# The beginning of a hybrid decoder step: input rows in one queue, cached pages gathered ahead of the memory turns, queries rotated by transfers

## What is computed

```python
xn = rmsnorm(x, g_attn)
cq, ckv, kr, ... = split(xn @ w_in)          # query and key-value compressions, rotary key, ...
q = (rmsnorm(cq, g_q) @ w_uq)                # 8 heads x (128 + 64)
q_rope = rope(q[..., 128:], pos)             # x1*cos - x2*sin, x1*sin + x2*cos
q_lat = einsum('bshn,rhn->bshr', q[..., :128], w_uk)
c_kv, k_rope = rmsnorm(ckv, g_kv), rope(kr, pos)
# sample tokens attend over 2048 cached positions each, found through page_table
past_lat, past_rope = cache_lat[page_table], cache_rope[page_table]
mem_k, mem_v = rmsnorm(mem, g_mem) @ w_mk, rmsnorm(mem, g_mem) @ w_mv
# ... a gated linear recurrence, cross attention to mem_k, mem_v, then 32 experts (top 4 of 32)
```

## Time and profile before

| | us |
|---|---|
| median of 3 runs (lowest, highest) | 1360.05 (1359.65, 1361.78) |
| the profiled execution's own time | 1358.12 |
| its span, from the first instruction to the last | 1356.3 |
| PE busy | 1304.1 (96%) |
| DVE busy | 364.0 (27%) |
| ACT busy | 253.4 (19%) |
| POOL busy | 101.4 (7%) |

### The profile page before, as it was taken

The page is one execution under the profiler, slowest core; times in us unless marked ns, Lnnn a source line. Parts: engine busy times, 40 slices in busy tenths (PEclk is TensorE's granted clock), DMA queues, the critical chain, the costliest instruction groups (busy, mean ns, idle before and its releaser), DMA issues.

```text
span 1356.3 us, 17073 instructions
## 1 busy us (share of the span) xinstructions
PE 1304.1 (96%) x6899; PEld 692.5 (51%) x6899; DVE 364.0 (27%) x796; ACT 253.4 (19%) x566; POOL 101.4 (7%) x133
## 2 busy tenths in 40 slices
PE   9999999999999999999998998989999998998988
PEld 7848887788887344344243433424434343342433
DVE  3864433211456222113021111202212112120212
ACT  4314345221125111011110101101011011010102
POOL 2652221001200000000000000000000000000000
PEclk9999999999999999999999989999999999999999
DMA  9894567548969999999999999999999999999996
GB/s 325 285 363 156 202 242 246 197 145 309 293 234 377 389 417 426 429 428 429 428 429 429 429 428 428 428 429 423 430 428 430 427 430 428 431 427 428 430 425 263
DMA packets 64898, 499.03 MB, mean 368 GB/s; under 512 B 5967, under 2 KB 7352, under 8 KB 39768
## 3 DMA queue, kind: packets, MB, share of 16 engines
q1 hardware_dynamic: 51424, 453.37, 81.1%
q0 software_dynamic: 13216, 44.50, 9.7%
q10 hardware_dynamic: 216, 0.58, 0.1%
HBM read 491.34 MB, written 7.08 MB: 367 GB/s over the span
## 4 chain that ended last, share of the span: by engine, by line
PE 75%; DMA 20%; DVE 1%; POOL 1%; issue 1%; SPq 0%; ACT 0%; ACTq 0%; DVEq 0%; POOLq 0%
PE bank L1348 22%; PE bank L804 17%; PE bank L1368 13%; DMA arena<-in_w_down 10%; DMA ring<-in_w_gate_up 9%; PE bank L1401 4%; PE bank L1332 4%; PE bank L754 1%; PE bank L1357 1%; PE bank L838 1%; PE bank L1363 1%; PE bank L1285 1%; PE bank L1182 1%; PE bank L767 1%; DMA ring<-in_cache_kv_latent,arena 1%
## 5 line engine op out<-in xcount | busy, mean ns | idle before, releaser
L1348 PE MATMUL bank<-ring,arena 128*64 128x512 f32 x1536 | 344.8, 597 | 6.4 <-DMA ring<-in_w_gate_up 6.4
L1368 PE MATMUL bank<-arena 128*64 128x512 f32 x1000 | 229.3, 609 | 30.2 <-DMA arena<-in_w_down 30.2
L804 PE MATMUL bank<-arena,ring 128*128 128x264 f32 x1008 | 230.7, 388 | 0.0
L1348 PEld LDWEIGHTS bank<-ring,arena 128*64 128x64 f32 x1536 | 104.3, 137 | 222.4 <-issue 206.9
L804 PEld LDWEIGHTS bank<-arena,ring 128*128 128x128 f32 x1008 | 189.4, 190 | 36.0 <-issue 4.4
L1368 PEld LDWEIGHTS bank<-arena 128*64 128x64 f32 x1000 | 70.4, 140 | 173.9 <-issue 129.0
L2607 DVE TENSOR_TENSOR resid<-resid,bank 128x264 f32<-128x264 f32 x128 | 54.8, 429 | 355.0 <-PE bank L1401 353.5
L1348 PE MATMUL bank<-arena 128*64 128x512 f32 x512 | 115.5, 593 | 3.5 <-DMA arena<-in_w_gate_up 3.5
L2612 DVE TENSOR_SCALAR arena<-bank 128x512 f32<-128x512 f32 x32 | 22.0, 688 | 340.8 <-PE bank L1348 340.8
L1566 ACT ACTIVATE arena<-bank 128x264 f32<-128x264 f32 (+6 forms) x129 | 51.0, 403 | 165.9 <-PE bank L804 126.8
L1946 ACT COPY arena<-bank 64x512 f32<-64x512 f32 x63 | 36.5, 580 | 232.9 <-PE bank L1368 232.1
(11 more groups left out here) (364 smaller groups left out, 933.2 us busy)
## 6 DMA issues: line engine op xcount, KB each, us to landing
ring<-in_w_gate_up SPq DMA_DIRECT2D x94, 2048.0 KB, 28.9
arena<-in_w_down SPq DMA_DIRECT2D x62, 2048.0 KB, 22.2
arena<-in_w_gate_up SPq DMA_DIRECT2D x32, 2048.0 KB, 28.8
ring<-in_w_in SPq DMA_DIRECT2D x10, 2048.0 KB, 11.4
out<-arena POOLq DMA_DIRECT2D x8, 512.0 KB, 5.0
ring<-v_rows POOLq DMA_DIRECT2D x8, 512.0 KB, 6.0
ring<-in_w_o_mla SPq DMA_DIRECT2D x2, 2048.0 KB, 8.9
ring<-in_w_o_gla SPq DMA_DIRECT2D x2, 2048.0 KB, 15.2
```

Of the source, the lines that this page charges most:

```text
L804: mm = nc.tensor.matmul(lin_bank(name)[0:m, 0:width], w(ring_name, nk, cols)[:, k, a:a + m], rhs[:, k, 0:width], start=(k == 0), stop=(k = ...
L1348: mm = nc.tensor.matmul(B[i // 2][CAP * (i % 2):CAP * (i % 2) + CAP, :], xg[:, k, CAP * e:CAP * e + CAP], slot(n)[:, a:a + 512], start=Fal ...
L1368: mm = nc.tensor.matmul(bank[CAP * half:CAP * half + CAP, :], hidden[:, k % 4, CAP * (k // 4):CAP * (k // 4) + CAP], weights[:, 512 * half ...
```

## The change

- The first two tiles of input rows are issued by SP, one behind the other, ahead of every weight; PE transposes tile 0 in all 8 chunks, and then tiles 1 and 2. There are 5 + 4 products of zeros in place of 12 + 3.
- The constants that the page numbers need are loaded ahead of `m_tok`, the others later. `page_rows` and the `idx` instructions move from the memory turns to the middle of the input products. The gathers wait for `idx`, for the transposes of `x_tok` and for its sums of squares, no longer for the last memory turn. `m_tok` moves to another place in SBUF.
- The sets come in the order 0, 4, 7, 1, 2, 3, 5, 6, 8 to 15. DVE turns the first behind the copy of `m2`, the second behind that of `uk0`, the third behind the rotated key, the fourth behind the second scaling, and three more ahead of the copies of the spread queries.
- The four products `rot0` to `rot3` and their ACT copies go. SP copies `q_pairs` into `q_turned` with halves of 32 partitions exchanged, four transfers of 32 partitions; the sign is in the table `sin`.
- `mk2` is multiplied ahead of `qb` instead of behind it. The weight `mk` is loaded ahead of `uq`.
- POOL clears `q_blocks` and `past_wide` (DVE before), loads seven small weights behind the first four sets (ahead of them before), and stores the latents behind all 16 sets (behind the eighth before).

```diff
             sp.dma_start(C[:, 0:P], consts[:, 0:P]).then_inc(S("units_loaded"), 16)
-            sp.dma_start(x_tok[:, 0, :], x_prompt[0, 0:P, :]).then_inc(S("x_loaded"), 16)
+            for tt in range(2):
+                sp.dma_start(x_tok[:, tt, :], x_prompt[0, P * tt:P * tt + P, :]).then_inc(S("x_loaded" if tt else "first_x_loaded"), 16)
             for n, (name, _) in enumerate(RING):
+                if name == "gq":
+                    lin_done(sp, "qr3")
+                    for i in range(4):
+                        j = i ^ 1
+                        sp.dma_start(q_turned[32 * i:32 * i + 32, :, :], q_pairs[32 * j:32 * j + 32, :, :]).then_inc(S("q_swapped"), 16)
...
                 if name == "in_a":
+                    sp.dma_start(table[:, 0:N_PAGES - KEPT], consts[:, KEPT:N_PAGES]).then_inc(S("mem_loaded"), 16)
+                    sp.dma_start(m_tok, mem_prompt[0].rearrange("(t p) d -> p t d", p=P)).then_inc(S("mem_loaded"), 16)
                     sp.dma_start(C[:, P:KEPT], consts[:, P:KEPT]).then_inc(S("const_loaded"), 16)
-                    sp.dma_start(m_tok, mem_prompt[0].rearrange("(t p) d -> p t d", p=P)).then_inc(S("mem_loaded"), 16)
-                    sp.dma_start(table, consts[:, KEPT:]).then_inc(S("const_loaded"), 16)
                     sp.dma_start(wuk, w_uk[0].rearrange("r h n -> r (h n)")).then_inc(S("uk_loaded"), 16)
+                    sp.dma_start(table[:, N_PAGES - KEPT:], consts[:, N_PAGES:]).then_inc(S("const_loaded"), 16)
...
             pool.wait_ge(S("idx"), 2)
-            pool.wait_ge(S("turn_full"), TI["m7"] + 1)
-            for n in range(16):
-                if n >= 4:
-                    pool.wait_ge(S("keys_turned"), n - 3)
-                gather_past(n, True)
...
+            pool.wait_ge(S("x_turned"), KC)
+            pool.wait_ge(S("token_sums"), 3)
+            for i, n in enumerate(KEY_ORDER):
+                if i >= 4:
+                    pool.wait_ge(S("keys_turned"), i - 3)
+                gather_past(n, True, i % 4)
+                if i == 3:
+                    load_small_weights()
+                if i == 7:
+                    lin_full(pool, "qr3")
+                    nc.gpsimd.memset(q_blocks, 0.0)
+                    nc.gpsimd.memset(past_wide, 0.0).then_inc(S("q_copies"), 1)
...
             pe.wait_ge(S("dve_step"), 1)
-            zero_products(12)
+            zero_products(5)
...
-            zero_products(3)
-            pe.wait_ge(S("x_loaded"), 48)
+            zero_products(4)
+            pe.wait_ge(S("first_x_loaded"), 16)
             for c in range(KC):
                 if c >= 6:
                     turned(pe, f"gains{c - 6}")
-                for tt, (t0, n) in enumerate(TILES):
+                nc.tensor.transpose(X_BANK[c][:, 0:P], x_tok[:, 0, c * P:(c + 1) * P], ident)
+            pe.wait_ge(S("x_loaded"), 32)
+            for c in range(KC):
+                for tt, (t0, n) in list(enumerate(TILES))[1:]:
                     mm = nc.tensor.transpose(X_BANK[c][:, t0:t0 + n], x_tok[0:n, tt, c * P:(c + 1) * P], ident[0:n, 0:n])
                 mm.then_inc(S("x_turned"), 1)
...
             input_half("kr", C_KR, ROPE, 0)
+            pe.wait_ge(S("x_copied"), KC)
+            pe.wait_ge(S("pages"), 1)
+            pe.wait_ge(S("mem_loaded"), 32)
+            nc.tensor.matmul(SCORE_BANK[:, 0:16], con("spread", 16), pages[0:16, :], start=True, stop=True).then_inc(S("page_rows"), 1)
             w_ready(pe, "in_a")
...
-            for j in range(4):
-                lin_done(pe, f"qr{j}")
-                lin(f"rot{j}", [(con("rot"), q_pairs[:, j, :])], T)
...
-            project(["mk1"], "mk", 8, 512, memT, NMEM, first=P)
+            project(["mk1", "mk2"], "mk", 8, 512, memT, NMEM, first=P)
...
             memory_turned(2)
+            turn_keys(0)
             turn_out("uk0", [(ukT[:, 0:512], P, (0, 512))])
...
+            turn_keys(1)
             memory_turned(4)
             memory_turned(6)
             scale_by_rms(3, cq, cq, "g_q", 2, T, 256, rstd)
...
+            lin_done(dve, "qr3")
+            dve.wait_ge(S("q_swapped"), 64)
             V.tensor_tensor(q_pairs, q_pairs, bc(con("cos")[:, None, :], [P, 4, T]), ALU.mult)
```

More of the change, by code:

```diff
@@ L90, in constants @@
     put("cos", np.tile(np.cos(ang), (4, 1)))
-    put("sin", np.tile(np.sin(ang), (4, 1)))
+    put("sin", np.concatenate([-np.sin(ang), np.sin(ang)] * 2))
     put("carry", np.tile((np.arange(PROMPT) % CH != 0).astype(f), (P, 1)))
@@ L100, in constants @@
     put("within", (i % 8).astype(f)[:, None] + np.array([0, 0.5], f))
-    pick = np.zeros((8, 8, 32), f)
-    for b in range(8):
-        pick[b, b] = 1
-    put("pick", pick.reshape(8, 256))
     return c
@@ L118 @@
 LIN = (["cq0", "cq1", "ckv", "kr", "rotk", "mk0"]
-       + [f"qn{h}" for h in range(8)] + [f"qr{j}" for j in range(4)] + [f"rot{j}" for j in range(4)]
-       + [f"ql{h}" for h in range(8)] + ["mk1", "qb", "own0", "own1", "mk2", "mk3", "mv0", "mv1"]
+       + [f"qn{h}" for h in range(8)] + [f"qr{j}" for j in range(4)]
+       + [f"ql{h}" for h in range(8)] + ["mk1", "mk2", "qb", "own0", "own1", "mk3", "mv0", "mv1"]
        + ["ga"] + EARLY[0:2] + [f"la{h}" for h in range(4)]
@@ L158 @@
 N_DOWN = NE - 1
+KEY_ORDER = (0, 4, 7, 1, 2, 3, 5, 6) + tuple(range(8, 16))
 PADS, LOW = 8 - TOPK, -3.0e38
@@ L940, in _ @@
             turned(pe, "krt")
-            project(["mk2", "mk3"], "mk", 8, 512, memT, NMEM, first=2 * P)
+            project(["mk3"], "mk", 8, 512, memT, NMEM, first=3 * P)
             past_scores(0)
@@ L1630, in _ @@
             turn_out("krt", [(kr_tok[:, 0:2, :], P, (0, 128)), (kr_tok[0:8, 2, :], 8, (128, 192))])
-            for j in range(4):
-                out(f"rot{j}", q_turned[:, j, :])
             for h in range(H_MLA):
@@ L1635, in _ @@
             out("mk1", memk[:, 1, :], width=NMEM)
+            out("mk2", memk[:, 2, :], width=NMEM)
             lin_full(act, "qb")
@@ L2100, in memory_turned @@
                     .then_inc(S("turned_by_dve"), 1)
+            dve.wait_ge(S("page_rows"), 1)
+            for i in range(2):
+                V.tensor_scalar(idx[:, :, i, :], SCORE_BANK[:, 0:16].rearrange("p (r b) -> p r b", r=2), con("within")[:, i:i + 1], 2.0, ALU.add, ALU.mult).then_inc(S("idx"), 1)
             inverse_of_rows_at_start(5, [(slice(3, 5), P)])
@@ L2161, in _ @@
                                 bc(krT[half, PROMPT:T, None], [64, 8, 4]), ALU.mult).then_inc(S("q_sample"), 1)
[L2162 removed]
+            turn_keys(5)
+            turn_keys(6)
+            lin_done(dve, "mk2")
             lin_full(dve, "qb")
+            dve.wait_ge(S("q_copies"), 2)
             for dst, src in wide_past_queries(0) + wide_past_queries(1)[:2]:
```

104 lines of the change are left out of this document (44 added, 60 removed).

## The result

| | us |
|---|---|
| before, median of 5 runs on the same chip | 1359.65 (1358.72 to 1361.78) |
| after, median of 5 runs | 1365.89 (1365.78 to 1366.81) |
| ratio | 1.0046, 95% interval 1.0032 to 1.006 |
| after, profiled execution | 1366.79, span 1364.9 |

The changed kernel is slower by 0.46%, 6.2 us, outside the predicted range. PE's timeline shows where it goes: `mk0` stands where it was forecast, and the loss that was not forecast comes behind it. `past_scores(0)` begins at 76.83, where before it began at 68.97.

The account below looks back on a forecast made before the run. PE's instruction stream bounds the trunk, weight loads the experts, which shift with it. +3.05 at `mk0` (head start included) and -1.87 for rotation make +1.2 us: 1360.05 to 1361.2, range 1357.3 to 1363.8.

Parts of the forecast that it names:

- The transfers: Four copies of `q_pairs` inside SBUF, costed at nothing: PE's work ahead of `qb` leaves 7.3 us to hide them.
- The start: PE's input products begin at 10.3 in place of 12.3: -2.0 us, bounds 0 and -2.5.
- The gathers and `mk0`: First gather at 19.7, second rotary gather landed at 34.5, `mk0` at 36.9 in place of 33.85: +3.05 us.
- The rotation products: The eight records of `rot0` to `rot3` leave PE's stream: -1.87 us.
- POOL's clearing: POOL's clearing of 3,584 columns, hidden by the same stretch of PE's work ahead of `qb` as the transfers.
- The other key sets cost nothing: On DVE, four of eight sets are turned before the scaling's end; only one is left before `past_scores(0)`: no cost.
- key sets in time: Rival for the memory turns: second rotary gather there by 31.3, `mk0` at 33.7, -2.0 us, 1358.0; chance 0.2.
- a POOL held up by DVE: Rival: gathers slip 1.9 us each beside DVE's scaling, `mk0` at 38.8, sum +3.1, 1363.1; chance 0.17.
- The start gives nothing: Rival: `in_a` lands two us later behind the tiles, everything from `page_rows` on slips, about +2.4, 1362.5; chance 0.08.
- rotated queries later than `mk2`: Sign against the forecast, ahead of `qb`: the rotated queries are ready only after the `mk2` products; no size given.

Follow-up runs that it names:

- the run in which the engines were quiet: The changed kernel with the gathers of the last two key sets ahead of `past_scores(0)` held back until the transfers landed: 1361.49, ratio 1.0015.

## Why the prediction was wrong, step by step

**The transfers** are the step that failed: "I cost them at nothing, and any us over 7.3 falls on the path." The cover was right. `qb` starts at 66.03 where `mk2` ended at 63.33; the transfers, issued from 52.33, had DVE waiting until 62.20, 9.9 us, which is 2.6 over the 7.3, and PE's wait ahead of `qb` was 2.70. The price was wrong: it was set by small stores of 2.7 us, met by the 2.4 us of the run in which the engines were quiet, and not by the 8.2 to 8.6 us that gathers took beside other loads. The prediction looked at what stood ahead of them in SP's queue, found it issued long before, and took it for landed: `gv0` landed at 60.0 (29.33 and 30.7), where in the kernel before, with the later gathers, it landed at 50.3 (28.74 and 21.6). And a wait there costs more than itself: DVE's key sets and copies queue behind it (+1.96), and PE's clock falls (+1.69).

**The start**, "-2.0 us (bounds: 0 ... -2.5)", is a size: -1.1 at the first product, and behind it 1.37 lost to the clock and 0.32 to the moved `page_rows`. The turns of the rows set the beginning, not the first half of `in_a`, which landed at 10.5 (10.3 forecast): the last sixteen took 3.57 us, 0.22 each, where the earlier trace rows gave 0.18. The clock was no term of the sum.

**The gathers and `mk0`**: the first gather at 21.12 (19.7 forecast), the second rotary gather's landing at 34.4 (34.5), its turn from 34.54 to 35.21 (34.5 to 35.2), `mk0` at 36.90 (36.9). The numbers agree by luck. The first gather came 1.4 us late and the way from there to the landing was 1.5 shorter than the forecast's; and with the head start gone PE stood 2.70 us, not 5. DVE was the releaser, as forecast, but waited only 0.77 us for pages; the rest is its own work. Where it waits for none, as in the repeat of the changed kernel, the two key sets still cost 1.5 us (`uk0` to `mk0` 5.60 in place of 4.11).

**The rotation products** gave 1.78 of their 1.87 us, and **POOL's clearing** (51.94 to 55.06) hid behind the same stretch. "The other key sets cost nothing" held until the late rotation put key sets 5 and 6, next in DVE's order, into the time in which `qb` was to be copied.

**The rivals**: key sets in time did not occur, nor a POOL held up by DVE: the two gathers beside DVE's scaling of the memory tiles (TENSOR_SCALAR, from 21.38) kept it 1.13 and 1.10 us. The slow gather of the earlier trace rows is there again, 2.65 us at 73.69, beside the same TENSOR_TENSOR scaling (73.21, 2.32 us). "The start gives nothing" came true in its result, no head start at `uk0`, by another cause. None had the transfers, though the prediction named "rotated queries later than `mk2`" as what would make it wrong.

## What to carry to other kernels

A transfer that replaces work of the engine on the path should be priced by the loads and gathers that move at that moment, by the landing of the last one issued ahead of it and not by its issue; here 2.4 us became 5 to 8. When one part of a change starts transfers earlier, look what other part issues into them. And where a stretch of PE's work is only reordered, allow for its clock: in the kernel with the start alone a saving of 1.1 us was turned into a loss of 0.6 by it.

## What the runs showed of the hardware

Copies of 32 partitions to 32 others in SBUF (132 KB, four at once) moved 217 GB/s at 96% of the DMA engines, about half of what loads moved at that share. Their landing was 2.4 us with quiet engines, 5.0 to 6.9 beside gathers alone, 6.0 to 6.8 behind a 2 MB load and the last gathers, 5.8 to 7.8 with more gathers beside, and a queue of their own (4.5 to 6.8) had them land no earlier. The 2 MB load `gv0` took 19.8 to 24.9 us to landing in five profiles with the late gathers of before, and 24.8 to 33.4 in thirteen with the early ones. The granted clock fell from 1.00 to 0.50 between 9.8 and 12 us in the middle of work with PE's busy share at 1.00, for 3.4 to 6.8 us, in 8 of 10 profiles of one order of turns, and in 1 of 6 with 0.6 us of products of zeros put between; why is open. A gather beside a TENSOR_TENSOR scaling of 2.3 us on DVE kept POOL 2.2 to 3.1 us, one beside TENSOR_SCALAR scalings 1.10 to 1.14.
